# 160 instead of 144 gathered tokens, low halves held behind one-hots, and the gate product of a chunk in one operation

## The reference, cut to what matters

```python
def peer_block(tok, wq, keys, u, v):
    qr = (tok @ wq).reshape(p, 8, 2, 128)
    s = einsum('phcd,hckd->phck', qr, keys)             # 2 x 128 sub-keys per head
    top_s, top_i = top_k(s, 16)
    cand = top_s[:, :, 0, :, None] + top_s[:, :, 1, None, :]
    ids  = top_i[:, :, 0, :, None] * 128 + top_i[:, :, 1, None, :]
    best, j = top_k(cand.reshape(p, 8, 256), 16)        # 8 heads x 16 experts per token
    eidx = take_along_axis(ids, j);  g = softmax(best)
    act = gelu(einsum('phkd,pd->phk', u[eidx], tok))
    return einsum('phk,phkd->pd', g * act, v[eidx])
```

## Time and profile before

| | us |
|---|---|
| median of three runs | 1956.92 |
| span of the profiled execution | 1955.2 |
| TensorE busy in it | 1926.3 |
| VectorE busy | 1491.8 |
| GpSimd busy | 885.0 |
| ScalarE busy | 865.3 |

### The profile page before, as it was taken

The page is one execution under the profiler, slowest core; times in us unless marked ns, Lnnn a source line. Parts: engine busy times, 40 slices in busy tenths (PEclk is TensorE's granted clock), DMA queues, the critical chain, the costliest instruction groups (busy, mean ns, idle before and its releaser), DMA issues.

```text
span 1955.2 us, 34516 instructions
## 1 busy us (share of the span) xinstructions
PE 1926.3 (99%) x12628; PEld 1215.0 (62%) x12628; DVE 1491.8 (76%) x2955; ACT 865.3 (44%) x1315; POOL 885.0 (45%) x558
## 2 busy tenths in 40 slices
PE   9999999999999999999999999999999999999997
PEld 7647777777777776555556666655555555555554
DVE  7975566555365668999899999951899888899885
ACT  6444446655443333333356666653333333333331
POOL 3732222221333454676877767775344442344320
PEclk9999999999999999999999999999999999999998
DMA  5622113223342223776989999986999999899971
GB/s 201 226 95 98 46 60 123 91 85 132 121 158 87 95 69 116 235 280 248 355 281 364 372 364 370 363 279 233 361 398 400 387 357 347 337 393 385 372 270 49
DMA packets 161051, 469.37 MB, mean 240 GB/s; under 512 B 17368, under 2 KB 59360, under 8 KB 160424
## 3 DMA queue, kind: packets, MB, share of 16 engines
q1 hardware_dynamic: 81824, 240.98, 33.7%
q0 software_dynamic: 41728, 151.03, 21.0%
q10 hardware_dynamic: 37384, 75.84, 10.5%
HBM read 402.98 MB, written 64.80 MB: 239 GB/s over the span
## 4 chain that ended last, share of the span: by engine, by line
PE 79%; DVE 15%; issue 2%; POOL 2%; ACT 1%; DMA 1%; ACTq 0%; DVEq 0%; POOLq 0%; SPq 0%
PE ps L2311 28%; PE ps L1854 27%; PE ps L1973 10%; PE ps L1870 3%; DVE rows L1640 2%; PE ps L2127 1%; POOL w_lo L588 1%; PE ps L2251 1%; PE ps L2252 1%; DVE eq L1627 1%; DVE eq L1625 1%; PE ps L2330 1%; DVE hot L1706 1%; PE ps L2107 1%; PE ps L2185 1%
## 5 line engine op out<-in xcount | busy, mean ns | idle before, releaser
L588 POOL TENSOR_TENSOR w_lo<-raw,w_hi 128x1024 bf16<-128x1024 f32 x229 | 508.5, 2225 | 642.7 <-ACT w_hi L698 619.8
L698 ACT ACTIVATE w_hi<-raw 128x1024 bf16<-128x1024 f32 x357 | 374.5, 1051 | 364.4 <-PE ps L2311 190.3
L1854 PE MATMUL ps<-act_hi,w_hi 128*128 128x432 bf16 (+1 forms) x1040 | 358.2, 346 | 0.7 <-DVE proj L1205 0.7
L1854 PE MATMUL ps<-act_lo,w_hi 128*128 128x432 bf16 (+1 forms) x1040 | 358.3, 346 | 0.0
L1854 PE MATMUL ps<-act_hi,w_lo 128*128 128x432 bf16 (+1 forms) x1040 | 358.3, 346 | 0.0
L2311 PE MATMUL ps<-W_hi,w_hi 128*128 128x432 bf16 x992 | 343.4, 346 | 0.8 <-issue 0.8
L2311 PE MATMUL ps<-W_hi,w_lo 128*128 128x432 bf16 x992 | 343.4, 346 | 0.0
L2311 PE MATMUL ps<-W_lo,w_hi 128*128 128x432 bf16 x992 | 343.4, 346 | 0.0
L621 POOL DMA_INDIRECT rows<-in_v_units,rowi x128 | 168.9, 1320 | 314.5 <-DVE accS L1751 296.4
L1058 ACT ACTIVATE hb<-ps 128x432 f32<-128x432 f32 x128 | 68.0, 531 | 310.0 <-PE ps L1854 306.2
L1726 DVE TENSOR_TENSOR w_lo<-raw,w_hi 128x1024 bf16<-128x1024 f32 x124 | 151.5, 1221 | 52.5 <-ACT w_hi L698 52.3
(11 more groups left out here) (454 smaller groups left out, 3396.5 us busy)
## 6 DMA issues: line engine op xcount, KB each, us to landing
raw<-in_u_units SPq DMA_DIRECT2D x128, 512.0 KB, 4.9
raw<-in_v_units SPq DMA_DIRECT2D x128, 512.0 KB, 10.0
raw<-in_units SPq DMA_DIRECT2D x99, 512.0 KB, 3.2
hd<-hb ACTq DMA_DIRECT2D x128, 224.0 KB, 5.5
Hb<-hd SPq DMA_DIRECT2D x32, 896.0 KB, 8.2
gd<-gsb ACTq DMA_DIRECT2D x48, 448.0 KB, 6.9
Gb<-gd SPq DMA_DIRECT2D x32, 672.0 KB, 6.5
gz<-stage ACTq DMA_DIRECT2D x24, 288.0 KB, 2.1
```

The lines of the kernel that those rows point to most:

```text
L588: pool.tensor_tensor(w_lo[:, k % RING, :], raw[:, k % RAW, :], w_hi[:, k % RING, :], ALU.subtract).then_inc(lo_ready, 1)
L698: act.activation(w_hi[:, k % RING, :], raw[:, k % RAW, :], ACT.Copy).then_inc(hi_ready, 1)
L1854: last = pe.matmul(ps[:, bank + half, 0:n], w[:, slot, col:col + P], x(k)[:, half * n:(half + 1) * n], start=(k == 0 and w is w_hi and x i ...
```

## The change

`NX` goes from 16 to 32: 160 tokens are gathered, 416 stay dense. Every matmul of the U and V phases has 416 columns in place of 432, and there are 52 gate steps in place of 54. The 32 `x_dot`s move from the V phase to VectorE's list ahead of the first gate product; their gathers move into GpSimd's U loop, three to a chunk from chunk 113 on (`X_FETCH`), each behind the low half of that chunk. The 32 `x_combine`s stand after every third chunk from 8 on. In the gate bodies GpSimd's low half of unit c+8 waits for a number of finished `one_hots`, `hots_at(c)`. The last fetches of u rows come at chunk 108 on, not 114. `Gb` gets all 8 blocks, the last two by a DMA from `gsb`, so `gated` is one operation over 448 columns. `W_hi` and `W_lo` lose 32 columns.

```diff
-NX = 16
+NX = 32
-X_DOT, X_GELU, X_COMB = 4, 64, 72
+X_FETCH, X_COMB, X_STEP = 113, 8, 3
+HOTS_AHEAD = 2
 def row_chunk(s):
-    return J_END * BODY + 2 + (d - during) // 2
+    return J_END * BODY - 4 + (d - during) // 2
+def hots_at(c):
+    body, k = divmod(c - J_G * BODY, BODY)
+    return body * G_BODY + k + HOTS_AHEAD if c > J_G * BODY else 0
 ...
-        W_hi = sb("W_hi", [P, RING, TD], BF16)
+        W_hi = sb("W_hi", [P, RING, TDX], BF16)
-        Gb = [sb("Gb0", [P, NBK, GRP, TBLK], F32)]
+        Gb = [sb("Gb0", [P, NBLK, GRP, TBLK], F32)]
 ...
             def load_gh(g, pg, need):
+                sp.dma_start(Gb[pg][:, NBK:NBLK, :, :].rearrange("e b c t -> e b (c t)"),
+                             gsb[:, :, bass.ds(g * GRP, GRP), :].rearrange("e b c t -> e b (c t)")).then_inc(gh_in[pg], 16)
 ...
             for c in range(NCH):
                 if c + RING < NCH:
+                    if 0 < hots_at(c) <= N_STEP:
+                        pool.wait_ge(b_hot, hots_at(c))
                     low_half(U_PEER + RING + c, U_PEER + RING + c)
 ...
+                for i in [i for i in range(NX) if min(X_FETCH + i // 3, NCH - 1) == c]:
+                    if i == 0:
+                        pool.wait_ge(rowx_known, 1)
+                    fetch_v(n_dot(i), a["u_rows"], rowx[:, i:i + 1])
 ...
-            act.wait_ge(comb_done, n_dot(NX - 1) + 1)
+            act.wait_ge(comb_done, NX)
             act.activation(xtab[:, 1, :], xtab[:, 0, :], ACT.Gelu_apprx_tanh).then_inc(x_acts, 1)
 ...
-                dve.tensor_tensor(out[:, 0:NBK, :], h[:, 0:NBK, :], Gb[g % 2][:, :, k, :], ALU.mult)
-                dve.tensor_tensor(out[:, NBK:NBLK, :], h[:, NBK:NBLK, :], gsb[:, :, c, :], ALU.mult).then_inc(w_mul, 1)
+                dve.tensor_tensor(out, h, Gb[g % 2][:, :, k, :], ALU.mult).then_inc(w_mul, 1)
+            for s in range(NX):
+                x_dot(s)
+            dve.wait_ge(b_prod, N_STEP)
             for c in range(NCH + LAG):
                 if c < NCH:
                     gated(c)
```

More of the change, by code:

```diff
@@ L127 @@
 N_MD, N_MA = 9, 8
-def extras_before(c, first):
-    return min(max((c - first + 1) // 2, 0), NX)
 def n_main(c):
-    return c + extras_before(c, X_DOT) + extras_before(c, X_COMB)
+    return NX + c + min(max((c - X_COMB + X_STEP - 1) // X_STEP, 0), NX)
 def n_dot(i):
-    return n_main(X_DOT + 2 * i) + 1
+    return i
 def n_comb(i):
-    return n_main(X_COMB + 2 * i) + 1
+    return n_main(X_COMB + X_STEP * i) + 1
 def attention_items():
@@ L290, in program @@
         maskneg = sb("maskneg", [P, P], BF16)
+        iota_at = used[0]
         iota = sb("iota", [P, P], F32)
@@ L295, in program @@
         rx = sb("rx", [P, 2, NTT], F32)
+        tails_at = used[0]
         tails = sb("tails", [P, 2, KT, 3], F32)
@@ L401, in program @@
         iota2 = sb("iota2", [P, P, 2], BF16)
+        IOTA_END = used[0]
         rowf_at = used[0]
@@ L415, in program @@
         rowx = sb("rowx", [P, XHALF], U32)
-        xtab = sb("xtab", [P, 3, XHALF], F32)
-        sel = sb("sel", [P, NX], F32)
+        xtab = place("xtab", iota_at, [P, 3, XHALF], F32)
+        sel = place("sel", tails_at, [P, NX], F32)
         assert used[0] <= nc.sbuf_usable_end, used[0] - nc.sbuf_usable_end
         used[0] = LATE
-        W_hi = sb("W_hi", [P, RING, TD], BF16)
-        W_lo = sb("W_lo", [P, RING, TD], BF16)
-        Gb = [sb("Gb0", [P, NBK, GRP, TBLK], F32)]
+        W_hi = sb("W_hi", [P, RING, TDX], BF16)
+        W_lo = sb("W_lo", [P, RING, TDX], BF16)
+        Gb = [sb("Gb0", [P, NBLK, GRP, TBLK], F32)]
         Hb = [sb("Hb0", [P, GRP, TD], F32)]
         wb = sb("wb", [P, 2, TD], F32)
-        assert used[0] <= HOT_END
+        assert used[0] <= IOTA_END
         fin_y = place("fin_y", ARENA, [P, KT, T], F32)
@@ L430, in program @@
         used[0] = ACT_HI
-        Gb.append(sb("Gb1", [P, NBK, GRP, TBLK], F32))
+        Gb.append(sb("Gb1", [P, NBLK, GRP, TBLK], F32))
         Hb.append(sb("Hb1", [P, GRP, TD], F32))
@@ L623, in fetch, with fetch_v @@
                     .then_inc(rows_in[s % RG], 16)
+            def fetch_v(n, table, index):
+                fetch(NST + n, table, (comb_done, n - RG + 1) if n >= RG else (dot_done, NST + n - RG + 1), index)
             v_rows = a["v_units"].rearrange("c e d -> (c e) d")
@@ L639, in _ @@
                     pool.dma_start(xin[to:to + NX, :, :], xpair[at:at + NX, :, g * NX:(g + 1) * NX]).then_inc(x_moved, 16)
-            def fetch_v(n, table, index):
-                fetch(NST + n, table, (comb_done, n - RG + 1) if n >= RG else (dot_done, NST + n - RG + 1), index)
-            for c in range(NCH):
-                fetch_v(n_main(c), v_rows, rowi[:, c:c + 1])
-                i = (c - X_DOT) // 2
-                if c == X_DOT + 2 * i and 0 <= i < NX:
+                for i in [i for i in range(NX) if min(X_FETCH + i // 3, NCH - 1) == c]:
                     if i == 0:
@@ L650, in _ @@
                     fetch_v(n_dot(i), a["u_rows"], rowx[:, i:i + 1])
-                i = (c - X_COMB) // 2
-                if c == X_COMB + 2 * i and 0 <= i < NX:
+            for c in range(NCH):
+                fetch_v(n_main(c), v_rows, rowi[:, c:c + 1])
+                i = (c - X_COMB) // X_STEP
+                if c == X_COMB + X_STEP * i and 0 <= i < NX:
                     fetch_v(n_comb(i), v_rows, rowx[:, i:i + 1])
@@ L1137, in v_body @@
                     w_high(i * RING + (k - 2), (k - 2) % RING)
-            with act.Fori(1, X_GELU // RING) as i:
-                v_body(i)
-            act.wait_ge(comb_done, n_dot(NX - 1) + 1)
+            act.wait_ge(comb_done, NX)
             act.activation(xtab[:, 1, :], xtab[:, 0, :], ACT.Gelu_apprx_tanh).then_inc(x_acts, 1)
-            with act.Fori(X_GELU // RING, NCH // RING) as i:
+            with act.Fori(1, NCH // RING) as i:
                 v_body(i)
@@ L1760, in x_dot @@
                     dve.wait_ge(x_kept, 2)
+                    dve.wait_ge(dot_done, NST)
                 dve.tensor_tensor_reduce(out=row, in0=row, in1=x_rep[:, :], scale=1.0, scalar=0.0, op0=ALU.mult, op1=ALU.add,
@@ L1784, in gated @@
                 if k == 0:
-                    dve.wait_ge(gh_in[g % 2], 32 * (g // 2 + 1))
+                    dve.wait_ge(gh_in[g % 2], 48 * (g // 2 + 1))
                 if c >= 2:
@@ L1804, in _ @@
                 combine(s)
-                i = (s - X_DOT) // 2
-                if s == X_DOT + 2 * i and 0 <= i < NX:
-                    x_dot(i)
-                i = (s - X_COMB) // 2
-                if s == X_COMB + 2 * i and 0 <= i < NX:
+                i = (s - X_COMB) // X_STEP
+                if s == X_COMB + X_STEP * i and 0 <= i < NX:
                     x_combine(i)
```

11 lines of the change are left out of this document (5 added, 6 removed).

## The result

The changed kernel takes 2008.61 us, the median of four runs (2003.67 to 2011.63); the kernel before took 1957.24 us beside it (1955.56 to 1957.82, four runs). The ratio is 1.0262, with a 95% interval from 1.0249 to 1.0275: 51 us slower. I had forecast 1984 us, and 1960 to 2008 as the forecast's own range: the direction was right, about half of the loss was missing, and the time lies just above the range. The profiled execution has a span of 2008.4 us, 26.1 us over the 1982.3 that my sum gave for it.

The account below looks back on a forecast made before the run. TensorE was taken as the bound from 1015.67 us, VectorE's chain before. V start +44.5, V phase -20.6, clock +1.7 and DMA +1.5 on 1955.2 gave 1982.3, or 1984 us as run median; range 1960 to 2008, 8 in 10 1940 to 2008.

Parts of the forecast that it names:

- The loop of gathers: Gate bodies: one-hots, held low half, gather, landing, dot product, one-hots; two steps take L + 6.54 us, 6.62 us per step.
- the pile in front of V: GpSimd from chunk 113: 11 low halves at 2.28 us and 31 gathers at 1.45 us before the last gather starts.
- the price of the transfers in V: V phase: 399 GB/s asked after the change; 6.6 us more if 392 were the ceiling, otherwise nothing; taken as 1.5 us.
- the landing time L in the loop: Gate bodies: time from a gather's issue until its row lands, taken as 6.7 us, between 6.3 and 7.3.
- the end of U: After the last gate step at 1312.2 us: twenty chunks without gates in 84.4 us, so U ends at 1396.6 us.
- The start of the gates: Step 2 of the gates: two of four low halves wait for its one-hots, so it starts at 986.9 us, -3.8 us.
- The gap in front of V: Between U and V: TensorE waits for GpSimd's gathers and low halves and the last extra dot product, 22.8 us.
- The V phase and what follows: V to the kernel's end: 3072 narrower matmuls save 20.6 us; clock adds 1.7 us, DMA 1.5 us, the end nothing.
- a case in which the clock falls in the bodies: Rival, gate bodies: waits bring half clock; if half of 24 pairs of steps were hit, +29 us, 2013 us; chance 0.11.
- The one-hots get the gain: Rival, gate bodies: the loop does not bind, TensorE sets 5.74 us per step, total 1941 us; chance 0.14.
- The point that I named: Gate bodies: whether gathered rows land within 4.9 us of issue, which decides if the loop is longer than TensorE's two steps.
- The extras hide as well: Rival, end of U: no gap from the extras, with the loop also absent, 1941 - 22 = 1919 us; chance 0.05.

Follow-up runs that it names:

- a1: The changed kernel without the wait for one-hots in front of the low halves: 1966.19 us, ratio 1.0051.
- a2: The changed kernel with the hold kept for low halves, but each held chunk's gathers issued ahead of its low half: 1956.92 us, ratio 1.0002.
- e1: The kernel before the change with only the hold of the low halves behind one-hots added: 2000.87 us, ratio 1.0238.
- c3: The changed kernel with HOTS_AHEAD 3 in place of 2, each low half held one step more: 2253.97 us, a single run.
- b2: The changed kernel with the last 11 low halves made by VectorE between its extra dot products, not by GpSimd: 1998.8 us, ratio 1.0213.
- a4: The changed kernel without the extras' 32 gathers of u rows and 32 dot products (a constant instead, result wrong): 1986.79 us, ratio 1.0159.
- a3: The changed kernel without the DMA copy from `gsb` to `Gb`, the gate product again in two operations: 1994.9 us, ratio 1.0193.
- c2: The changed kernel with HOTS_AHEAD 1 in place of 2, each low half held one step fewer: 1962.23 us, ratio 1.0037.
- b3: The changed kernel with held chunks' gathers first, no gate copy (two gate operations), and the last 11 low halves on VectorE: 1928.05 us, ratio 0.9857.
- d1: As b3, but the extras' gathers start at chunk 110 instead of 113, with 14 low halves on VectorE: 1930.51 us, ratio 0.987.
- c1: The changed kernel with the gate copy kept but unused, the gate product again in two operations: 2007.27 us, ratio 1.0267.

## Why the forecast had the direction and half the size

The loop of gathers, the pile in front of V and the load on the DMA engines in V are there, each shown by an experiment that takes it away. What failed are three steps of the sum: the price of the transfers in V, put at 1.5 us and worth some 12; the landing time L in the loop, put at 6.7 us and measured at 7.2; and the end of U, where I had put nothing on top of 20 undisturbed chunks and ScalarE's waits for loads, with the half clock after the last of them, cost most of 8.8 us. The 26.1 us between my sum and the span come apart as 12.3 + 9.0 + 8.8 + 0.1 - 4.2, to 0.1.

**The start of the gates: 4.2 us better.** Step 2's one-hots were done at 982.74 us, not 986.9. The two low halves that stay took the first one-hot operation to 5.00 us and no further, as worked out; I had placed it at the time it has in the trace of before, and it started 3.8 us earlier (976.01 against 979.80 in the earlier trace rows). Why is not shown. It is not the fewer columns alone: in traces of other kernels with 416 columns it starts between 977.0 and 979.6 us, so this term is in good part scatter. What the hold does to the operation is shown: in a1, without it, the operation took 8.34 us, in a2 and e1, with it, 5.02.

**The loop of gathers: 9.0 us worse.** I took L = 6.7 us, halfway between two measured values, on the argument that a slower pace relieves the transfers. The trace has a median of 7.2 at a DMA share of 0.90 (7.3 over the stretch of the earlier trace rows), no less than before at 0.99. With 7.2 the formula gives 6.87 us per step, measured 6.80, forecast 6.62. The form of the loop, two steps in L + 6.54 us, holds, in e1 to 0.03 us and in c3 over one step to 0.2. In the prediction the Trainium skill (DMA: Bandwidth & Descriptors, "Anatomy of one DMA") gave 3.2 us for a 512 KB DMA by its fit, an estimate, by which the loop would not bind. The trace goes against it for gathers that share the engines: none landed in under 5.1 us. Its rule may hold for a DMA alone; no run here shows one.

**The end of U: 8.8 us worse, a term that I did not have.** From the end of step 51 (1317.0) to the end of U (1410.2) there are 20 chunks, 84.4 us by my reckoning; they took 93.2. The first is 1.5 us longer than 4.22, at half clock, after the waits of the last steps. The next 14 take 4.22 us each, and 7.1 us are in the last five, from 1382 us on. I had counted GpSimd's pile as something that delays only the extras. But a load of a unit waits for the low half four units earlier, the low halves stood in the pile, and the DMA engines were full: from the first low half to the last gather's issue it took 74.2 us (1345.74 to 1419.93), against 59.1 us for TensorE's last 14 chunks. So ScalarE waited for loads, its GELUs stood behind, TensorE waited 3.11 us, and ran at half clock after it, which made the last chunk 3.1 us longer. The pile alone is not the cause: in b2, without it, the wait for loads does not go, it becomes 15.7 us long, at 410 GB/s. Of two of these waits, 5.93 us here and 15.7 in b2, the load is the one behind the first group of `Gb` and `Hb`.

**The gap in front of V: 22.9 us, forecast 22.8.** That it fits to 0.1 us is luck: two errors cancelled in it. The pile started 0.2 us later than worked out and took 74.2 us from its first low half, 4.1 more than the 70.1 worked out (a gather every 1.60 us, not 1.45, since (74.2 - 11 x 2.24)/31 = 1.60), and the dot product of the last gather started 10.1 us after its issue where I had 6.7; together 7.7 us. Against that stand 0.5 us less between this dot product and V, and TensorE, which came late itself by the 7.1 us told above. a4 shows that the extras are the whole of it: 0.8 us without them. The Trainium skill (SBUF — State Buffer, "Who interferes with whom") says that a VectorE instruction with two SBUF inputs contends with a GpSimd instruction that reads SBUF. The trace agrees: the dot product at 1363.86 us took 3.85 us beside a low half, the one at 1430.05, with none beside it, 1.23.

**The V phase and what follows: 12.3 us worse, the largest term.** In the 124 chunks V took 537.2 us, where 2976 matmuls at 175.8 ns and my 3.2 us for clock and transfers make 526.4; the other 1.5 us lie behind them. The clock cost 1.5 us (first chunk 5.71 us), as forecast, so the step that failed is the price of the transfers: I allowed 1.5 us, with 6.6 as the price if 392 GB/s were the ceiling, and they cost 12 (537.2 against 525.3 in a3). Between nothing and 6.6 I took the value nearer to nothing, and the 392 was the highest rate that a row showed, which is not what the engines keep up. In the stretches 1560 to 1700 and 1700 to 1840 us the kernels with the copy (all but c3, whose V phase lies later) move 377 (c2) to 391 GB/s (b2), and those without it (a3, b3, d1) 381 to 391, all at a share of 0.99 to 1.02. The rates are the same; what differs is what a chunk of 4.22 us asks for, 399 GB/s with the copy and 385 without (1.68 and 1.62 MB). Without it TensorE never waits in V; with it, used or not (after, c1), it does. A stretch that already has a share of 1.01 has no room for the 57 KB per chunk that the copy adds, 3.4% of 1.68 MB.

**The clock.** I gave 0.11 to a case in which the clock falls in the bodies. It fell to 0.95 on the mean there, but TensorE was waiting for the loop anyway, whose pace fits without it; what can be read as its cost is the 1.5 us in the first chunk behind the gates, and 3.1 us in the last chunk of U.

**The rivals.** "The one-hots get the gain" did not come true with the gathers behind the low halves; a2 shows what it is worth once they are ahead of them. The point that I named, rows within 4.9 us of their issue, decided it. Of the signs that I gave, VectorE's wait for rows (over 80 us: 99.0) came in, TensorE's for the one-hots (some 40: 31.5) and the distance of the bodies (about 46 us: 7 x 6.80 = 47.6) nearly, as did an idle piece of some 20 us in front of V (22.9); a V matmul every 175.8 ns did not (537.2/2976 = 180.5). "The extras hide as well" does not come true even in b3 and d1, since the transfers take over.

## What to carry to other kernels

A wait put in front of one instruction holds back everything behind it in its engine's list; before it is added, the lead of each prefetch behind it is to be read from the trace, from issue to use, and set against the landing time under load. If the lead goes, the prefetch moves ahead of the wait: here that turned a loss of 42 us into a gain of 9. An edit that saves an operation by adding a transfer is to be priced at the engine that is full: at a DMA share of 1.00 a copy of 3.4% more bytes made 525 us into 537, and the operation that it saved gave nothing that could be measured. And two errors that cancel in one term can look like a good forecast: the gap in front of V fitted to 0.1 us with three of its inputs off.
